# A head's scores moved ahead of both halves of its V projection, in a float32 decoder trunk on one core

## The reference, cut to what matters

```python
kv = rmsnorm(x, kv_norm) @ w_kv                 # 2048 x 12288: K and V of three groups
parts = rmsnorm(x, b_norm) @ b_w_in             # 2048 x 8192: Q of three groups, and z
for g, (window, dil) in enumerate(((128, 1), (512, 4), (2048, 16))):
    s = q[g] @ k[g].T * 128 ** -0.5 + bias[g]   # masked to the group's keys
    # softmax over the keys, weighted sum of v[g]; groups merged by their denominators
y = merged * silu(z)
x = x + y @ b_w_out                             # then a final rmsnorm
```

## Time and profile before

| | |
|---|---|
| median of 3 runs | 1441.41 us |
| the profiled execution | 1441.45 us |
| its span | 1439.6 us |
| granted clock, mean | 0.998 |
| PE busy | 1420.8 us (99%) |
| DVE busy | 897.1 us (62%) |
| ACT busy | 719.9 us (50%) |
| POOL busy | 386.5 us (27%) |

### The profile page before, as it was taken

How to read it: one execution, slowest core, us unless ns; L and a number is a source line. 1 busy time by engine, 2 the same in 40 slices (tenths; PEclk the granted TensorE clock), 3 DMA queues, 4 the chain that set the end, 5 groups by cost and what they waited for, 6 DMA issues and landing times.

```text
span 1439.6 us, 23832 instructions
## 1 busy us (share of the span) xinstructions
PE 1420.8 (99%) x8901; PEld 1307.5 (91%) x8901; DVE 897.1 (62%) x1508; ACT 719.9 (50%) x1167; POOL 386.5 (27%) x170
## 2 busy tenths in 40 slices
PE   6999999999999999999999999999999999999997
PEld 6999999988899989999899998999989999899886
DVE  3899999632556566565665656656566565665633
ACT  6444444675654454444544445445454454544643
POOL 6888888888300000000000000000000000000785
PEclk9999999999999999999999999999999999999999
DMA  9666766556696567665666666666666666665652
GB/s 276 187 191 182 196 181 195 185 177 216 182 273 187 157 186 191 182 186 162 186 187 182 186 166 186 182 183 186 170 186 179 182 187 173 186 176 168 235 192 87
DMA packets 455087, 268.37 MB, mean 186 GB/s; under 512 B 4491, under 2 KB 437211, under 8 KB 454668
## 3 DMA queue, kind: packets, MB, share of 16 engines
q1 hardware_dynamic: 454572, 267.01, 64.9%
q10 hardware_dynamic: 480, 0.90, 0.2%
HBM read 263.60 MB, written 4.29 MB: 186 GB/s over the span
## 4 chain that ended last, share of the span: by engine, by line
PE 97%; ACT 1%; DVE 1%; issue 0%; ACTq 0%; DVEq 0%
PE bank L438 14%; PE bank L434 14%; PE bank L435 7%; PE bank L437 7%; PE bank L409 6%; PE bank L407 6%; PE bank L408 6%; PE bank L442 6%; PE bank L443 6%; PE bank L444 6%; PE bank L462 4%; PE bank L464 4%; PE bank L463 4%; PE bank L1478 1%; PE bank L1493 1%; PE bank L1462 1%
## 5 line engine op out<-in xcount | busy, mean ns | idle before, releaser
L372 POOL TENSOR_TENSOR w_lo<-raw,w_hi 128x1024 fp32r<-128x1024 f32 x159 | 381.7, 2411 | 1027.0 <-ACT w_hi L363 1026.5
L363 ACT ACTIVATE w_hi<-raw 128x1024 fp32r<-128x1024 f32 x382 | 399.2, 1060 | 416.1 <-PE bank L444 130.6
L372 DVE TENSOR_TENSOR w_lo<-raw,w_hi 128x1024 fp32r<-128x1024 f32 x224 | 268.3, 1222 | 187.4 <-ACT w_hi L363 185.4
L442 PE MATMUL bank<-mem_a,w_hi 128*128 128x256 f32 x768 | 216.0, 281 | 1.7 <-DVE mem_a L969 1.6
L443 PE MATMUL bank<-mem_a,w_hi 128*128 128x256 f32 x768 | 214.5, 279 | 0.0
L444 PE MATMUL bank<-mem_a,w_lo 128*128 128x256 f32 x768 | 213.4, 278 | 0.0
L434 PE MATMUL bank<-mem_b,w_hi 128*128 128x512 f32 x512 | 203.6, 398 | 0.0
L438 PE MATMUL bank<-mem_b,w_hi 128*128 128x512 f32 x512 | 202.5, 396 | 0.0
L997 DVE SCALAR_TENSOR_TENSOR bank<-u,taps,bank 128x256 f32<-128x256 f32 x448 | 179.5, 483 | 1.4 <-ACT bank L708 1.4
L407 PE MATMUL bank<-w_hi,mem_a 128*128 128x384 f32 x512 | 171.3, 335 | 0.0
L409 PE MATMUL bank<-w_hi,mem_a 128*128 128x384 f32 x512 | 171.3, 334 | 0.0
(11 more groups left out here) (199 smaller groups left out, 2429.2 us busy)
## 6 DMA issues: line engine op xcount, KB each, us to landing
raw<-w_kv_dram SPq DMA_DIRECT2D x96, 1024.0 KB, 6.1
raw<-b_w_in_dram SPq DMA_DIRECT2D x64, 1024.0 KB, 7.3
raw<-a_w_in_dram SPq DMA_DIRECT2D x47, 1024.0 KB, 5.8
raw<-a_w_out_dram SPq DMA_DIRECT2D x16, 1024.0 KB, 5.1
raw<-b_w_out_dram SPq DMA_DIRECT2D x16, 1024.0 KB, 5.4
bias<-bias_dram SPq DMA_DIRECT2D x16, 384.0 KB, 6.4
x_sb<-x_dram SPq DMA_DIRECT2D x4, 512.0 KB, 5.5
resid_dram<-x_sb SPq DMA_DIRECT2D x1, 2048.0 KB, 10.2
```

Of the source, the lines that this page charges most:

```text
L363: nc.scalar.activation(w_hi[:, stream.half_slot(half), :], raw[:, slot, part:part + HALF], ACT.Copy).then_inc(hi_done, 1)
L372: eng.tensor_tensor(w_lo[:, stream.half_slot(half), :], raw[:, slot, part:part + HALF], w_hi[:, stream.half_slot(half), :].bitcast(F32), A ...
L442: nc.tensor.matmul(dst[:, 0:S], wide_hi, source(kt, 0), start=(kt == 0), stop=False)
```

## The change

`scores(h)` is called ahead of both calls of `project_v` instead of between them. Nothing else differs: the same instructions, in another order, on PE alone. `mm_done` is counted by `project_v` as before, and `scores_done` by scores.

```diff
             def head_values_and_scores(h):
 
+                scores(h)
                 project_v(pe, h, 0)
-                scores(h)
                 project_v(pe, h, 1)
```

## The result

The changed kernel takes 1443.49 us, the median of 20 runs (1443.0 to 1445.17), against 1441.36 for 20 runs of the kernel before (1440.93 to 1441.74): ratio 1.0018, 95% interval 1.0012 to 1.0025. I had forecast 1441.0 and a range that ended at 1442.2. The change makes the kernel slower by 2.1 us. That is less than the 2.9 us which the prediction said a measurement could not tell from no change; with 20 runs of each kernel the interval tells it. The 20 runs lie on two levels: 13 between 1443.0 and 1443.6, 7 between 1444.9 and 1445.2. The profiled execution took 1445.05.

A forecast was written before the change was run, and what follows sets the result against it. PE, busy 99% of the span, was taken to bound the kernel. Boundaries saving 0.02 to 0.03 us in 16 heads gave 0.4 less, all else 0: 1441.45 - 0.4 = 1441.05, forecast 1441.0, range 1440.2 to 1442.2.

The forecast's parts named there:

- PE bounds the kernel: Whole kernel: PE is busy 99% of the span, so only PE's own time or a wait put into PE moves the end.
- PE's own work: Matmul boundaries in each head: new order saves 0.02 to 0.03 us a head, times 16 = 0.3 to 0.5 us.
- Entering plain float32 from Z: Boundary Z to scores: entering costs 0; the rival, 0.08 us a head, adds 1.3 us, 1442.7, chance 0.07.
- The wait at scores: Scores right behind Z: last `q_lo` ends at 900.35, wanted at 902.20, 1.85 us to spare; cost 0.
- The rival that I held likeliest on the slow side: Stall at scores: PE stops once a head for late `q_lo` or its waits, 8.8 us in all, 1450.2; chance 0.04.
- the ripple over slab 0: ACT and DVE splits behind V0, 1.73 us later: cost 0; as rival, PE pays from 2.8 us more lateness, chance 0.02.
- Behind head 15, cost 0: Tail behind the last head: later `B_OUT` splits and `normalise`, tightest cover 1.3 us, all early enough; cost 0.
- if it hits an operation of POOL again, 1342.4 + 3.10 = 1345.5: Worst case for L1221 (`normalise`) behind head 15: ends at 1345.5, still early enough for `turn_probs`.
- L1221 takes about 1 us: Sign expected in the changed timeline behind head 15: `normalise` takes about 1 us, in a pause of POOL.
- the PE idle that I would have taken as proof against me: Sign against the forecast: a PE idle at scores named by L1171 or by ACT's L806.
- The price of a late DVE operand: Stall at scores, priced by PE's wait from L444 to L442: 0.55 us lost, times 16 = 8.8 us.

## Why the prediction was wrong

- **PE bounds the kernel, and only its own time or a new wait moves the end: right.** The loss is one new wait and, in some runs, the clock behind it.
- **PE's own work, 0.02 to 0.03 us a head less: right.** 60.16 became 60.14. Entering plain float32 from Z cost nothing (1.74 against 1.73), as the earlier trace rows had it.
- **The wait at scores has 1.85 us of cover: right.** PE starts scores at 901.93 with no idle, in every head. The rival that I held likeliest on the slow side did not happen, nor did the ripple over slab 0: ACT's next split now starts at 920.52, 0.2 behind V's end at 920.32, as before.
- **Behind head 15, cost 0: wrong, and this is the step that failed.** I had the right cover (1.3 us between L1221 and `turn_probs`), the right neighbour (POOL) and the rule that one blocks the other, and gave the meeting a wrong size: "if it hits an operation of POOL again, 1342.4 + 3.10 = 1345.5". Two things were wrong in that. The start: I let the eight y2 subtractions run as long as before, but they are exposed to POOL too; 7.15 instead of 4.97 us moved `normalise` to 1344.09. This one decided it: at their old length, from 1336.84 on, they would have ended near 1341.8 and `normalise` would have run from about 1342.0 to 1343.0, in POOL's pause from 1341.69 to 1343.66, as forecast (an estimate from these rows). And the length: I took the 3.10 seen before, where only one of the two instructions was held, as the worst case. ACT's next split now ended before POOL was through, POOL ran two without a gap, and each of the two DVE instructions was held by one: 4.99. It ended 3.1 us later than before (1349.08 against 1345.96) and was wanted 0.4 earlier; less the cover of 1.3 that is 2.3 us late. The sign "L1221 takes about 1 us" failed with it; the PE idle that I would have taken as proof against me I looked for at scores alone.
- **The chances.** The price of a late DVE operand was there only for scores in 16 heads. For the tail, where a release moved by 1.7 us beside a cover of 1.3, there was no rival at all.

What the rows say of DVE beside POOL: held were `tensor_scalar` (L1221, and before the change also L1213 on 128 x 2 elements, 1.24 us instead of the 0.17 it takes in the heads) and `tensor_tensor` with both inputs in SBUF (L1283). Not held was L1198, which reads PSUM (0.62 at 1333.61 beside POOL's three in the earlier trace rows, the same 0.62 at 1327.55 without). Inputs in SBUF alone do not make the difference: the two `tensor_reduce` (L1211) read only SBUF and take 1.40 us at 1335.19, beside POOL, as they do in the heads without it. The Trainium skill, "SBUF — State Buffer", SBUF: two separate sides, has DVE and GpSimd share one pair of ports as an exclusive lock: whichever starts first keeps it for its whole instruction, a GpSimd instruction, or a DVE instruction in a two-port mode or, against a GpSimd instruction that reads SBUF, with two SBUF inputs. The runs agree for the two SBUF inputs of L1283, 2.58 and 2.63 us in the changed kernel. L1221 has one beside its scalar per row, and took 2.37 and 2.70 us there. In the heads it takes 0.42 us for 384 columns and 0.62 for 768, 0.20 for 384 more, where `tensor_reduce` takes 0.54 and 0.94, 0.40 for as many. Twice the pace fits a two-port mode, but no run shows the mode itself.

## What to carry to other kernels

When a change moves a release on one engine, place every instruction behind it again, next to what the other engines do then; with DVE and GpSimd on SBUF, price the worst case as one whole GpSimd instruction for each DVE instruction of a kind that is held, not as the length once seen, and give the instructions ahead of it the same price. A tail that runs once behind a loop can cost more than all the iterations gain: here -0.02 us in each of 16 heads against a wait of 2.2 us once. If a result comes earlier, its consumers can be moved up into the idle time that it opens: that took the loss away here (1441.11). It gained nothing beyond that, for head 15 in the old order did as well (1440.97), and neither is faster than the kernel before by more than its interval.

## What the runs showed of the hardware that was not expected

- A pause of PE of 2.2 us (2.58 from the last start to the next) was followed by the lower clock in some executions: 7 of 20 of the changed kernel lie 1.6 us above the other 13, and the profiled one of them shows a granted clock of 0.55 for 1.71 us and 0.85 for 6.43 us. The profiled executions of the kernel with head 15 alone in the new order (1445.48) and of the one with the splits later (1445.52), with pauses of 2.20 and 2.15 us, show 0.54 and 0.51 right behind it. Where POOL waits, the profiled execution was one of the lower level (1443.32), and the clock stays 1.00 behind its pause of 1.62 us.
- DVE instructions of 0.41 us took 2.58 and 2.63 us beside POOL subtractions of about 2.5 us, two in a row, each held by a subtraction of its own.
- ACT multiplied the same 128 x 1152 elements in 1.44 us beside a POOL subtraction.
